# Three mixing stages of a 256-token block: recurrence steps issued inside a product, attention by pairs of heads, a gated branch that ends inside its product

## The reference

```python
def hgrn2(...):       # b = cumsum(log f), per chunk of the sequence
    scores = einsum('bhtk,bhtsk,bhsk->bhts', qt, exp(b_t - b_s), kt)      # causal
    o = rms_norm_f32(scores @ v + state part, norm_g) * silu(g)
def banded_attention(...):
    p = softmax(q @ k.T * scale + bias [, sink]);  out = p @ v
```

## Time and profile before

| | |
|---|---|
| median of 3 runs | 1920.85 us (1918.58 to 1935.26) |
| profiled execution, its own time | 1936.79 us |
| its span, first to last instruction | 1935.1 us |
| PE busy | 94% of the span |
| DVE, ACT, POOL busy | 59%, 49%, 5% |
| mean granted PE clock | 0.960 |
| DMA | 283.99 MB, 147 GB/s on average |

### The profile page before, as it was taken

How to read it: one execution, slowest core, us unless ns; L and a number is a source line. 1 busy time by engine, 2 the same in 40 slices (tenths; PEclk the granted TensorE clock), 3 DMA queues, 4 the chain that set the end, 5 groups by cost and what they waited for, 6 DMA issues and landing times. The chain is left out here.

```text
span 1935.1 us, 25833 instructions
## 1 busy us (share of the span) xinstructions
PE 1814.7 (94%) x9487; PEld 1517.1 (78%) x9487; DVE 1150.0 (59%) x1845; ACT 952.8 (49%) x1511; POOL 87.4 (5%) x107
## 2 busy tenths in 40 slices
PE   7969899999779998999998899999999997999999
PEld 7856688888668887888886678888888876678887
DVE  4363466677556657766634447666766634557665
ACT  4442364555655555545542536555545543336544
POOL 0052000000000000000002100000000001110000
PEclk9987999999899999999999999999999997899999
DMA  8410235556135554555642013555555660013652
GB/s 317 146 35 1 88 131 195 192 175 229 62 109 185 182 184 166 166 180 183 244 169 68 1 66 131 195 195 183 177 180 183 242 211 23 1 66 131 195 195 87
DMA packets 215656, 283.99 MB, mean 147 GB/s; under 512 B 9240, under 2 KB 149528, under 8 KB 215576
## 3 DMA queue, kind: packets, MB, share of 16 engines
q1 hardware_dynamic: 215576, 282.93, 43.7%
HBM read 281.81 MB, written 1.09 MB: 146 GB/s over the span
## 5 line engine op out<-in xcount | busy, mean ns | idle before, releaser
L927 PE MATMUL banks<-act_both,ring_hi 128*128 128x512 f32 x2112 | 750.4, 396 | 4.0 <-DVE act_both L570 1.6
L928 PE MATMUL banks<-act_both,ring_lo 128*128 128x256 f32 x2112 | 591.9, 280 | 0.0
L927 PEld LDWEIGHTS banks<-act_both,ring_hi 128*128 128x128 f32 x2112 | 396.8, 188 | 101.8 <-issue 4.1
L928 PEld LDWEIGHTS banks<-act_both,ring_lo 128*128 128x128 f32 x2112 | 396.8, 188 | 5.0
L1043 DVE TENSOR_TENSOR ring_lo<-weight_slots,ring_hi 128x1024 fp32r<-128x1024 f32 x240 | 283.4, 1222 | 61.9 <-ACT ring_hi L998 61.5
L313 DVE TENSOR_TENSOR ring_lo<-weight_slots,ring_hi 128x1024 fp32r<-128x1024 f32 (+3 forms) x150 | 170.8, 1150 | 163.6 <-ACT ring_hi L305 161.3
L998 ACT ACTIVATE ring_hi<-weight_slots 128x1024 fp32r<-128x1024 f32 x240 | 239.2, 1044 | 0.6 <-DMA weight_slots<-in_ffn_w 0.6
L305 ACT ACTIVATE ring_hi<-weight_slots 128x1024 fp32r<-128x1024 f32 (+3 forms) x150 | 146.9, 996 | 154.6 <-PE banks L698 148.5
L1012 ACT ACTIVATE normed<-banks 128x512 f32<-128x512 f32 x132 | 78.9, 598 | 283.8 <-PE banks L928 283.8
L696 PE MATMUL banks<-ffn_down_hi,ffn_hidden_hi 128*128 128x512 f32 x528 | 207.5, 393 | 0.4 <-DVE ffn_down_lo L1048 0.2
L697 PE MATMUL banks<-ffn_down_lo,ffn_hidden_hi 128*128 128x512 f32 x528 | 206.7, 392 | 0.0
(11 more groups left out here) (366 smaller groups left out, 2240.1 us busy)
## 6 DMA issues: line engine op xcount, KB each, us to landing
weight_slots<-in_ffn_w SPq DMA_DIRECT2D x44, 1024.0 KB, 6.7
weight_slots<-in_ffn_w_gate SPq DMA_DIRECT2D x44, 1024.0 KB, 5.4
weight_slots<-in_ffn_w_up SPq DMA_DIRECT2D x44, 1024.0 KB, 8.0
weight_slots<-in_ffn_w_down SPq DMA_DIRECT2D x88, 512.0 KB, 8.4
weight_slots<-in_ffn_w SPq DMA_DIRECT2D x44, 512.0 KB, 8.4
weight_slots<-in_ev_w_in SPq DMA_DIRECT2D x7, 2048.0 KB, 14.1
weight_slots<-in_od_w_in SPq DMA_DIRECT2D x5, 2048.0 KB, 9.3
weight_slots<-in_ab_w_in SPq DMA_DIRECT2D x5, 2048.0 KB, 12.8
```

The source lines that it names most:

```text
L927: pe.matmul(bank, k.hi(n)[:, q, :], k.act_both[:, q], start=q == 0, stop=False, skip_group_check=True)
L928: return pe.matmul(bank[:, 0:S], k.lo(n)[:, q, :], k.act_hi[:, q, :], start=False, stop=q == KD - 1, skip_group_check=True)
```

## The change

1. **Begin.** The small parameter loads are issued inside `begin`, between weight items 2 and 3. Item 0 comes in four pieces with a semaphore each. The column order of `ev_in` becomes forget logits, q, input, gate, q, k, forget bias (8 columns), v.
2. **Recurrence.** `hgrn` becomes class `Hgrn`, a side of product `ev_in`: the parameter products go behind part 3, its prologue behind parts 7 to 10, its nine rounds behind parts 9 to 20, its value products behind part 22; three level buffers in place of two pairs. `Fox` puts its logarithms behind part 31.
3. **Attention.** Class `Attention` works on pairs of heads, `fox` and the sparse layer use it. The two heads of a pair lie in rows 0 to 63 and 64 to 127 and their products alternate. POOL multiplies the probabilities themselves by the factor, so that PE transposes them against the identity (one record each). One score bank for each head of the pair, one transposition bank. In `fox` six of the output product's parts stand between the steps. No `keep_warm` in either. Latent and dilated attention keep `softmax_attention`.
4. **Odd layer.** The LRU steps move up by two or three parts, and square root, scan and product go behind parts 17 to 19. In `stick_breaking` the output part comes after `suffix` and `values`.

```diff
@@ begin
             for t in range(TT):
                 sp.dma_start(k.x[:, t], w["x"][0, P * t:P * t + P, :]).then_inc(k.x_loaded.sem, 16)
+            k.load_weights(sp, 2)
+            for dst, src in loads:
+                sp.dma_start(dst, src).then_inc(k.params_loaded.sem, 16)
             k.load_weights(sp, SLOTS)
@@ split_hi
-            if part.opens:
+            if part.item == 0:
+                act.wait_ge(self.first_in[n], 16)
+            elif part.opens:
@@ class Attention, tensor(pe, i): per step
+        d = self.duo_at(i)
+        if d >= 0:
+            flips(d, 0)
+        if i < self.duos:
+            scores(i)
+        if d >= 0:
+            flips(d, 1)
+        d = self.duo_at(i - 1)
+        if d >= 0:
+            values(d)
...
+            if d >= 1:
+                pe.wait_ge(*k.logits_ready.after(2 * d))
+            for t in range(TT):
+                keys = P * (t + 1)
+                for j in range(2):
+                    x, out = self.unit(d, j), self.scores_bank(j)[:, self.spots(t)]
+                    ins = pe.matmul(out, x["q"](t), x["kT"][:, 0:keys], start=True, stop="extra" not in x)
...
+            pe.wait_ge(*k.pool_a.after(n + 1))
+            if n >= 1:
+                pe.wait_ge(*(k.probs_T_ready.after(d + 1) if j else k.act_a.after(d)))
@@ vector(dve, i)
+        d = self.duo_at(i)
+        if d >= 0:
+            copy_even(d)
+        d = self.duo_at(i - 2)
+        if self.closes(d):
+            lower_part(self.pairs[d // G]["tile"])
+        if G == 1 and 1 <= i <= self.duos:
+            factors(i - 1)
+        if i < self.duos:
+            add_bias(i)
@@ scalar(act, i): copy_odd(d), exponentials(i), then the tile's act_hi; scale(pool)
+                    for t in range(TT):
+                        x = self.probs[:, (2 * (m * G + g) + j) % self.DEPTH, self.spots(t)]
+                        ins = pool.tensor_tensor(x, x, self.fac[:, m, j, t:t + 1].to_broadcast(list(x.shape)), ALU.mult)
+                    ins.then_inc(k.pool_a.sem, 1)
@@ class Hgrn
+    DIFF = {10: 0, 11: 1, 13: 2, 14: 3, 16: 4, 17: 5, 19: 6, 20: 7}
+    EXP = {11: 0, 12: 1, 14: 2, 15: 3, 17: 4, 18: 5, 20: 6, 21: 7}
+    ROUND = {9: 0, 10: 1, 11: 2, 13: 3, 14: 4, 16: 5, 17: 6, 19: 7, 20: 8}
+    KEEP = {13: 0, 14: 1, 15: 2, 17: 3, 18: 4, 20: 5, 21: 6, 23: 7, 24: 8}
...
+        if m in self.ROUND:
...
+                pe.wait_ge(*k.level_scaled.after(r))
+            if r >= 2:
+                pe.wait_ge(*k.level_kept.after(r - 1))
...
+        if m == 27:
+            act.wait_ge(*k.pe_b.after(1))
+            act.wait_ge(*k.bias_stored.after(16))
+            act.activation(self.o2, self.o, ACT.Square).then_inc(k.act_a.sem, 1)
@@ even_layer
+            product(k, block, "ev_in", KD, [feature(fa), feature(qa), token(ia), token(ga), feature(qb), feature(kb),
+                                            ("feature", lambda m: fb.unsqueeze(1), 8), token(vb)],
+                    side=Side(hgrn, fox), factors=[1.0] * 4 + [HD ** -0.5] + [1.0] * 3, then=None)
+            out = OutProduct(k, "ev_out", KD)
+            fox.end(block)
+            hgrn.end(block, (k.part_used, out.n0))
...
+        attend(k, block, att, out, {0: [0], 1: [1], 3: [2], 4: [3], 6: [4], 7: [5]}, {0: 4, 3: 6, 5: 8}, hgrn_ready)
@@ Lru.scalar, Lru.vector
+        if m == 17:
+            act.wait_ge(*k.dve_b.after(3))
+            act.activation(self.u, self.u, ACT.Sqrt).then_inc(k.act_b.sem, 1)
...
+        if m == 18:
             dve.wait_ge(*k.act_b.after(3 * NH + 3))
             k.dve.done(dve, dve.tensor_tensor(u, u, self.ig, ALU.mult))
             for t in range(NH):
                 ins = dve.tensor_tensor_scan(xc[:, t, :], self.a[:, t, :], u[:, t, :], 0.0, ALU.mult, ALU.add)
@@ stick_breaking, tensor
+            if 1 <= i <= H:
+                suffix(i - 1)
+            if i >= 2:
+                values(i - 2)
             if i in PARTS_AT:
```

More of the change, by code:

```diff
@@ new lines, in attend, with tile_waits, _ @@
+def attend(k, block, att, out=None, parts_at=None, split_at=None, other_tiles=None):
+    def tile_waits(pe, m):
+        for tile in (m // 2 * 2, m // 2 * 2 + 1):
+            if tile >= att.first_tile and tile - att.first_tile <= att.pairs[-1]["tile"]:
+                pe.wait_ge(*k.heads_done.after(tile - att.first_tile + 1))
+            else:
+                pe.wait_ge(*other_tiles)
+    @block.gpsimd
+    def _(pool):
+        att.scale(pool)
+    @block.tensor
+    def _(pe):
+        for i in range(att.steps):
+            att.tensor(pe, i)
+            for m in (parts_at or {}).get(i, ()):
+                tile_waits(pe, m)
+                out.part(pe, m)
+        if out:
+            tile_waits(pe, out.parts - 1)
+            out.last_parts(pe)
+    @block.vector
+    def _(dve):
+        for i in range(att.steps):
+            att.vector(dve, i)
+            if i in (split_at or {}):
+                k.split_lo(dve, out.n0 + split_at[i])
+    @block.scalar
+    def _(act):
+        for i in range(att.steps):
+            att.scalar(act, i)
+            if i in (split_at or {}):
+                k.split_hi(act, out.n0 + split_at[i])
+    att.passed()
@@ L1660, in even_layer, with __init__, start, _ @@
-def even_layer(k, loads, between):
-    with ExitStack() as ctx:
-        fb = ctx.enter_context(k.nc.sbuf_tensor("ev_fb", [8, S], F32))
+    def __init__(self, k, ctx, q, key, v, f, c):
+        self.k, self.q, self.key, self.v, self.f, self.c = k, q, key, v, f, c
+        self.one = ctx.enter_context(k.nc.sbuf_tensor("fox_one_hot", [self.H, self.H, P], F32))
+        self.lf = k.r_rows[0:self.H, :]
+    def start(self, block):
+        k, H = self.k, self.H
+        @block.gpsimd
+        def _(pool):
+            pool.tensor_copy(self.one[:], k.ident[0:H, 0:H].unsqueeze(2).to_broadcast([H, H, P]))\
+                .then_inc(k.fox_ready.sem, 1)
@@ new lines, in end, with _ @@
+    def end(self, block):
+        k, f = self.k, self.f
+        @block.vector
+        def _(dve):
+            dve.wait_ge(*k.act_b.after(1))
+            k.dve.done(dve, dve.scalar_tensor_tensor(out=f, in0=f, scalar=0.0, in1=self.lf, op0=ALU.min,
+                                                     op1=ALU.subtract))
+            k.dve.done(dve, dve.tensor_scalar(f, f, -1.0, None, ALU.mult))
+            dve.tensor_tensor_scan(self.c, k.ones[0:self.H, :], f, 0.0, ALU.mult, ALU.add).then_inc(k.fox_ready.sem, 1)
@@ L1671, in token @@
             return "token", lambda t: dst[:, t, :], HALF
-        stage, block = new_stage(k)
-        product(k, block, "ev_in", KD, [feature(qa), feature(fa), token(ia), token(ga), feature(qb), feature(kb),
-                                        token(vb), ("feature", lambda m: fb[:].unsqueeze(1), 8)], loads=loads)
-        stage.close()
-        between()
-        hgrn(k, qa, fa, ia, ga, key)
-        fox(k, qb, kb, vb, fb[:])
-        transpose_mix(k, range(NH))
+        with ExitStack() as early:
+            hgrn = Hgrn(k, early, qa, fa, ia, ga, key, params)
+            fox.start(block)
+            hgrn.start(block)
+            product(k, block, "ev_in", KD, [feature(fa), feature(qa), token(ia), token(ga), feature(qb), feature(kb),
[4 more added lines that the diff above has]
+            hgrn.end(block, (k.part_used, out.n0))
+            hgrn_ready = hgrn.passed()
+        k.act_b.passed(1)
+        fox_ready = k.fox_ready.after(2)
+        k.fox_ready.passed(2)
+        att = Attention(k, ctx, [dict(tile=p, first=True, last=True, units=[(fox.unit(2 * p), fox.unit(2 * p + 1))])
+                                 for p in range(fox.H // 2)], NH, banks=(6, 7, 4, 5), started=(fox_ready, k.product_copied.after(-3)),
+                        values_in=k.product_copied.after(0))
+        attend(k, block, att, out, {0: [0], 1: [1], 3: [2], 4: [3], 6: [4], 7: [5]}, {0: 4, 3: 6, 5: 8}, hgrn_ready)
+        out.weights(block)
 class Lru:
@@ L1823, in _, with end @@
             k.dve.done(dve, ins)
-            dve.tensor_tensor(g3[:], g3[:], xc[:], ALU.mult).then_inc(k.dve_b.sem, 1)
+        if m == 19:
+            dve.tensor_tensor(self.g3[:], self.g3[:], xc[:], ALU.mult).then_inc(k.dve_b.sem, 1)
+    def end(self, block, read):
+        k, g3 = self.k, self.g3
+        @block.scalar
+        def _(act):
+            act.wait_ge(*read)
+            act.wait_ge(*k.dve_b.after(4))
+            act.activation(k.act_hi[:, 0:NH, :], g3[:], ACT.Copy).then_inc(k.act_b.sem, 1)
+        @block.vector
+        def _(dve):
             dve.wait_ge(*k.act_b.after(3 * NH + 4))
@@ L2016, in odd_layer @@
         out = OutProduct(k, "od_out", KD)
-        ready = lru.end(block)
+        ready = lru.end(block, (k.part_used, out.n0))
         stick_breaking(k, block, lru.th[:].rearrange("p a b -> p (a b)"), qd, kd, vd, minus, shut, tri, out, ready)
```

799 lines of the change are left out of this document (487 added, 312 removed).

## The result

| | median | range | ratio to the kernel before (95% interval) |
|---|---|---|---|
| before | 1919.71 us | 1916.86 to 1935.26 | |
| after | 1875.24 us | 1867.70 to 1883.82 | 0.975 (0.9707 to 0.9794) |

The change makes the kernel 44.5 us faster. The forecast was 1842, with 1824 to 1866: the sign is right, and 33 us of the gain are missing. The profiled execution took 1875.61 us, its span is 1873.8.

A forecast was written before the change was run, and what follows sets the result against it. PE, busy 94% of 1935.1 us, was taken to bound the kernel. Even layer with start -52, sparse -24 and odd -3 sum to -79, a span near 1856; forecast 1842 us, range 1824 to 1866.

The forecast's parts named there:

- 47.2, against 73.7: Sparse layer: the new pairs' summed time in us against the old 24 softmaxes; with 2.5 for slow start, -24.
- so I take the difference and not the ratio: Whole kernel: profiled execution lay 0.8% above the median, so the -79 was taken as a difference, giving 1842 us.
- The start: Kernel start: PE's first product comes at 25.0 us, 8.9 later, as the first block's meeting waits for SP's loads.
- Rival (a): Kernel start: the meeting doesn't hold the product, PE starts near 12, 13 us better, 1829; chance 0.08.
- The product: Even product `ev_in`: its own 83.4 us plus 20.0 of added PE work and 5.9 of waits, ending at 134.3.
- rival (d): Even product: DVE and POOL's lock binds it, +12 us, 1854; chance 0.12.
- (e): Even product: recurrence rounds make PE wait, clock falls to 0.50, +98 us, 1940, slower than before; chance 0.03.
- The first 4 us after the pause run slower, 1.7: Forgetting attention and `ev_out`: the low clock after PE's pause costs only 1.7 us.
- (c): Sparse layer: the softmaxes stay at 1.2 GHz, +17 us, 1859; chance 0.10.
- Waits have a cover: Forgetting attention: a pair's 5 us chain is covered by two parts, or a part and the next scores.
- rival (b): Sparse layer: the halves of the PE array don't overlap, +11 us, 1853; chance 0.12.
- Odd layer: Odd layer: 5.5 us gained at the product's end, 3.5 lost in the product, -3 (-6 to +2).

The follow-up runs named there:

- e12b: The changed kernel unchanged, run once more: median 1871.90 us, ratio to the kernel before 0.9749.
- e1: The kernel before, unchanged, profiled a second time: 1925.86 us.
- e4: Changed kernel with the small parameter loads and weight items 2 and 3 issued at the start of the product's block, not in the first block: 1867.39 us.
- e2: Changed kernel with output parts 6 and 7 split a step later and the next feed-forward's first two parts split in step 7: 1862.16 us.
- e8: Changed kernel with the LRU steps and stick-breaking order of the kernel before: 1881.65 us.
- e11b: Changed kernel with late loads, splits ahead and grouped scores, plus output parts 2 and 3 one step earlier: 1838.52 us.
- e15: Changed kernel with five edits: loads late, splits ahead, scores grouped, idle products in the pause, output parts 2 and 3 earlier: 1837.21 us.
- e5: Changed kernel with grouped scores and the 8-row operands of the second products padded with zeros to 128 rows: 1860.39 us.
- e3: Changed kernel with a pair's 64-row score products all before its 8-row ones: 1859.99 us; one score term was lost for the first 128 queries.
- e9b: Changed kernel with three edits: loads late, splits ahead, scores grouped: 1843.59 us, ratio to the kernel before 0.9583.
- e10b: Changed kernel with late loads, splits ahead and grouped scores, plus ten idle products in PE's pause between product and attention: 1835.31 us.

## Why the prediction was wrong

The step that failed first of all is the cost of the even layer's attention stage: it was summed at full clock but for 1.7 us, and the clock took 17 us of it (point 5). Two terms of the new kernel were put at nothing, the waits behind the splits and the way to the feed-forward (points 5 and 6), and one stage of the kernel before was read from a long sample (point 1). Point by point, with e12b and e1 as typical traces of both kernels (spans 1874.4 and 1924.2, 49.8 apart):

1. **The basis.** The step that failed is the 73.7 in "47.2, against 73.7": it comes from a trace 11 us longer than e1's. The words "so I take the difference and not the ratio" did no harm: the ratio, 1856 to 1935.1, would have given 1842.5. The sparse attention (with the compressed part's last step) took 75.5 us there, 70.8 in e1 and 53.4 in e12b. The new pairs were sized well (49.7 forecast, 51.2 found); what they replace was read 4.7 us too long. Forecast -24, found -17.4. The other 7 of the 11 us lie in stages that aren't in the sum; between e1 and e12b those moved by 4 the other way.
2. **The start**: 25.0 forecast, 24.29 measured, 24.0 in e12b. That is 8 us later than before, and e4 shows the meeting as its cause. Rival (a) is out.
3. **The product**: 109.3 forecast, 107.2 to 107.8 measured. Of the 5.9 us of waits 3.6 came: 1.8 in the rounds (I took 4) and 1.8 before v (I took 1.9). The slow-down of DVE beside POOL was as in the earlier trace rows and had room, so rival (d) is out, and so is (e), at 0.97. The page that I cited of the Trainium skill (SBUF — State Buffer, SBUF: two separate sides) says that the two exclude each other for whole instructions. The trace agrees: beside POOL a split takes 1.1 us longer (4.53 for two), and PE's 1.8 us of waits in the rounds are the most that this cost.
4. **Pause**: 2.4 us in place of 4.2, transposes at 133.6 in place of 138.5.
5. **Attention and `ev_out`**: the step that failed is "The first 4 us after the pause run slower, 1.7". The stage holds 46 to 47 us of work at 2.4 GHz (63.3 x 0.73 in e12b), as summed; the clock took 17 us, not 1.7. Although the row of this stage before the change said 0.76, I had costed everything else at 1.00. Half clock was among my rivals, but for the product (e), where it didn't come, and for the sparse layer (c), where it came for 16 us only. Besides, "Waits have a cover" failed: 4.63 us at the last values, and three waits of 0.67 to 0.74, 6.8 together where I took 1 for the first step. I had looked at the chain of a pair, not at what stands ahead of the small step in DVE's queue.
6. **The way to the feed-forward**: not in the prediction at all, +7.1 us. The splits that the old `out_product` made for the next stage had no one to make them. e2 shows this, and 3.7 us of the waits of point 5.
7. **Sparse layer**: overlap as taken (rival (b) out), sink pairs 4.4 us apart (4.3), others 2.6 to 3.8 (2.95), and 4 to 5 where the one kind follows the other. 16 us at half clock at its start cost little, since PE isn't the bound there (it waits 2.19 and 1.08 us for POOL's products between these pairs): rival (c) is out.
8. **Odd layer**: -3 forecast, -8.2 by e12b against e1, -6.3 by e8's trace. PE's waits at the product's end, 1.18 and 2.95 us, are the 4 to 5 forecast (1.18 and 8.78 before, as in e8). But the product lost under 1 us, not 3.5, and later steps gave some 2 more: its last such wait fell from 2.81 to 1.95.

In sum: even layer -52 forecast and -28.1 found (-4.9 by 2 to 4, +21.6 by 5, +7.1 by 6); sparse +6.6, odd -5.2, untouched stages +4: -79 + 23.8 + 6.6 - 5.2 + 4 = -49.8. The medians lie 44.5 us apart (48.6 in e12b's set), so up to 5 of the 33 us that are missing are scatter between executions, which no term of this sum explains. The odd layer's better result is luck for the total, since it hides 5 us of what the other terms missed.

**What stays open.** Why the clock falls in this stage. The traces show it in three places, though PE counts as full in them: behind PE's pause (filling it keeps 1.00 there, with grouped scores), in steps of scores, transposes and values with no output part, and behind alternating scores. But a place alone doesn't decide (e11b and e15 run the same steps at 1.00 and at half clock). Few rows in use are neither shown as a cause nor excluded: padding them shortened the fall behind the pause in one profile (e5), and the median didn't move. Which property of the work the chip reacts to no run here tells.

## What to carry to other kernels

Before a stage is costed at full clock, read its granted clock in the trace of before: if it is low there, new work of the same kind may pay it too (here 0.76 before and 0.72 after). Multiply busy time by clock when the sizes of two versions are compared. When a loop written out by hand takes the place of a common routine, list what that routine did for the next stage (here two parts split ahead), and for each small step that frees a bank, what stands ahead of it on its engine. Profile the kernel before twice: 11 of its 1924 us moved between two executions, 4.7 of them in a stage whose gain was to be summed.

## What the runs showed of the hardware

- Products of 64 rows in the upper and lower half of the array run at the same time: eight records in 0.93 us, as four. Products of 8 rows that lie in the same rows don't: 1.51 us for eight. Where each 64-row product is followed by an 8-row one no overlap is seen: 0.42 us from one product of 128 columns to the next. The Trainium skill (TensorEngine Tiling (Array Packing), Key Properties) has both, that tiles run in parallel and that a change of tiling mode drains the engine. The trace agrees with the first by 0.93 against 0.92 for half the work. The 1.8 us that grouping saves a pair fit the second, if 64-row and 8-row products are different modes; how much of them is drain is the estimate of e3, 1.15.
- A pause of PE of 2.4 us was followed by 9.9 us at 1.2 GHz with PE full (e9b), by 3.0 us where the 8-row products were padded (e5), and by none where idle products filled it (e10b).
- One and the same stage, of unchanged code, took 66.6, 70.1, 71.6 and 72.5 us in four profiles, by the granted clock alone.
